# Scores of an eight-level scan: 64x64 column tiles in two bursts per head, six homes for mixed operands, a compact score tile

## The reference

```python
def step(state, inp):
    qb, kb, fb, vb = inp
    b = jnp.cumsum(fb, axis=2)
    b_last = b[:, :, -1:, :]
    inter = jnp.einsum('nhtk,nhkv->nhtv', qb * jnp.exp(b), state)
    diff = b[:, :, :, None, :] - b[:, :, None, :, :]
    decay = jnp.exp(jnp.where(incl, diff, -jnp.inf))
    scores = jnp.einsum('nhtk,nhsk,nhtsk->nhts', qb, kb, decay)
    intra = jnp.einsum('nhts,nhsv->nhtv', scores, vb)
    new_state = (jnp.exp(b_last[:, :, 0, :, None]) * state
                 + jnp.einsum('nhsk,nhsv->nhkv', kb * jnp.exp(b_last - b), vb))
    return new_state, inter + intra
...
o2 = hgrn2_chunk_scan(jnp.concatenate([qh, rev(qh)], axis=0),
                      jnp.concatenate([k_f, rev(k_b)], axis=0),
                      jnp.concatenate([logf_f, rev(logf_b)], axis=0),
                      jnp.concatenate([vh, rev(vh)], axis=0))
o = o2[:B] + rev(o2[B:])
```

## Time and profile before

| | |
|---|---|
| median of 3 runs | 1886.5 us (1885.9 to 1886.76) |
| the profiled execution's time | 1885.56 us |
| its span | 1883.7 us |
| TensorE products busy | 1853.5 us, 98% of the span |
| TensorE weight loads | 1602.5 us, 85% |
| VectorE | 1401.9 us, 74% |
| ScalarE | 1042.4 us, 55% |
| GpSimdE | 331.4 us, 18% |
| chain that ended last | PE 83%, DVE 13%, ACT 2%, issue 2% |
| L2036 (level steps) in that chain | 2% |

### The profile page before, as it was taken

The page is one execution under the profiler, slowest core; times in us unless marked ns, Lnnn a source line. Parts: engine busy times, 40 slices in busy tenths (PEclk is TensorE's granted clock), DMA queues, the critical chain, the costliest instruction groups (busy, mean ns, idle before and its releaser), DMA issues.

```text
span 1883.7 us, 32317 instructions
## 1 busy us (share of the span) xinstructions
PE 1853.5 (98%) x11238; PEld 1602.5 (85%) x11238; DVE 1401.9 (74%) x2658; ACT 1042.4 (55%) x1817; POOL 331.4 (18%) x145
## 2 busy tenths in 40 slices
PE   9999999999999999999999999999999999999998
PEld 7877887788888889999999998888888888888887
DVE  7785566667655568898997678977999976666666
ACT  6666455656644466667555555565665543333333
POOL 0000000000000000000000168886777400000000
PEclk9999999999999999999999999999999999999999
DMA  6624655443455544443445445554444455555554
GB/s 217 224 78 148 216 174 178 145 146 124 146 189 189 187 147 157 147 135 124 136 145 175 155 143 181 186 189 152 162 157 161 155 187 192 196 191 191 196 193 156
DMA packets 86157, 314.11 MB, mean 167 GB/s; under 512 B 9568, under 2 KB 9696, under 8 KB 85856
## 3 DMA queue, kind: packets, MB, share of 16 engines
q1 hardware_dynamic: 86048, 312.65, 49.2%
HBM read 311.56 MB, written 1.05 MB: 166 GB/s over the span
## 4 chain that ended last, share of the span: by engine, by line
PE 83%; DVE 13%; ACT 2%; issue 2%; DMA 0%; SPq 0%; DVEq 0%; ACTq 0%
PE ps L424 24%; PE ps L409 14%; PE ps L2735 11%; PE ps L290 6%; PE ps L1967 6%; PE ps L2739 6%; PE ps L2537 3%; DVE wsplit L273 3%; PE ps L819 2%; PE ps L2036 2%; PE ps L2923 1%; DVE sq L2979 1%; PE ps L440 1%; ACT wsplit L267 1%; DVE work L2300 1%
## 5 line engine op out<-in xcount | busy, mean ns | idle before, releaser
L267 ACT ACTIVATE wsplit<-ring 128x1024 fp32r<-128x1024 f32 x572 | 603.8, 1059 | 450.5 <-PE ps L424 265.4
L273 DVE TENSOR_TENSOR wsplit<-ring,wsplit 128x1024 fp32r<-128x1024 f32 x440 | 541.5, 1235 | 304.8 <-ACT wsplit L267 303.8
L424 PE MATMUL ps<-wsplit,gsplit 128*128 128x512 f32 x1992 | 456.5, 390 | 0.0
L424 PEld LDWEIGHTS ps<-wsplit,gsplit 128*128 128x128 f32 x1992 | 373.2, 188 | 81.3 <-issue 4.0
L273 POOL TENSOR_TENSOR wsplit<-ring,wsplit 128x1024 fp32r<-128x1024 f32 x132 | 317.2, 2404 | 664.5 <-ACT wsplit L267 664.2
L2735 PE MATMUL ps<-hsplit,wsplit 128*128 128x512 f32 x1024 | 368.6, 403 | 0.0
L409 PE MATMUL ps<-wsplit,hsplit 128*128 128x512 f32 x1248 | 298.1, 394 | 4.5 <-DVE wsplit L273 3.4
L2739 PE MATMUL ps<-hsplit,wsplit 128*128 128x256 f32 x1024 | 286.4, 280 | 0.0
L409 PEld LDWEIGHTS ps<-wsplit,hsplit 128*128 128x128 f32 x1248 | 231.6, 188 | 55.5 <-DVE wsplit L273 7.3
L290 PE MATMUL ps<-hsplit,wsplit 128*128 128x256 f32 x1956 | 253.6, 287 | 2.6 <-DVE hsplit L340 1.5
L290 PEld LDWEIGHTS ps<-hsplit,wsplit 128*128 128x128 f32 x1956 | 239.8, 191 | 10.4 <-issue 4.5
(11 more groups left out here) (346 smaller groups left out, 1900.3 us busy)
## 6 DMA issues: line engine op xcount, KB each, us to landing
ring<-in_weights SPq DMA_DIRECT2D x572, 512.0 KB, 3.3
work<-in_weights SPq DMA_DIRECT2D x8, 512.0 KB, 5.8
...
```

Source lines behind the costliest of these rows:

```text
L267: act.activation(wsplit[:, n % RING, 0, :], slab(s), ACT.Copy).then_inc(S("split", "lead"), 1)
L273: eng.tensor_tensor(wsplit[:, n % RING, 1, :], slab(s), wsplit[:, n % RING, 0, :], ALU.subtract).then_inc(S("split", RESTS[stream][0]), 1)
L424: mm = pe.matmul(YR[:, tt, half * 512:(half + 1) * 512], gsplit[:, slot, b, tt * P:(tt + 1) * P], wsplit[:, n, a, half * 512:(half + 1) * ...
```

## The change

- The eight steps within the quadrants' halves (diagonal, levels 0 to 5, and level 6, which pairs the halves) are products of 64 keys and 64 queries: four for a step, two for each half of PSUM's partitions, into 128 columns. Steps 0 to 3 lie in bank 3, steps 4 to 7 in bank 5. TensorE does them in two bursts of 16 products, before slot 3 and before slot 6. The step across stays as it was, now before slot 7, into bank 3.
- Mixed operands have six homes instead of two, the four old half-homes as four whole ones and two more in `yb`.
- VectorE collects steps 0 to 6 in a 128x(2x64) tile `near`, the first with a copy, the others under 64-wide masks: two after growth 4, one after growth 5, one after growth 6, and three at the head's end, where the last keep was.
- ScalarE copies `near` into `sT` (two instructions, one for each half of the partitions), then step 7 directly out of PSUM (two more), then the step across.

```diff
@@ -181,7 +181,9 @@
     tab = carve(N_TABLE - N_EYES)
     sm = carve(N_SMALL)
     hT = carve(KC, T)
-    level_masks = carve(LEVELS, P, dt=I32)
+    level_masks = carve(LEVELS - 1, HD, dt=I32)
+    near = carve(2, HD)
+    pos[0] += LEVELS * P - LEVELS * HD - HD
     filt_sum = carve(2, D)
     filt_dif = carve(2, D)
     sub = carve(16, P)
@@ -1933,9 +1935,26 @@
     qa, kb = qakb[:, 0, :, :], qakb[:, 1, :, :]
     totals = [forget.rearrange("p a t -> p (a t)")] + [carve(3 * (T >> l)) for l in range(1, LEVELS)]
     sT = carve(TT, T)
-    mixed = merged[:, 0:4, :].rearrange("p (b x) t -> p b x t", b=2)
+    mixed = [merged[:, 2 * b:2 * b + 2, :] for b in range(4)] + [yb[:, 4 + 2 * b:6 + 2 * b, :] for b in range(2)]
     hv = yb[:, 0:4, :].rearrange("p (t a) n -> p t (a n)", t=TT)
-    diag = strided(sT, 0, [[T + P, 2], [1, P]])
+
+    def half(h2):
+        return slice(HD * h2, HD * h2 + HD)
+
+    def quadrants(keys, queries):
+
+        return strided(sT, HD * queries, [[T + P, 2], [1, HD]], HD * keys, HD)
+
+    across_bank = ps[:, 3, 0:T]
+
+    def level_tiles(k):
+        return ps[:, 3 + 2 * (k // 4), k % 4 * P:(k % 4 + 1) * P].rearrange("p (a c) -> p a c", a=2)
+
+    def mix_home(h, l):
+        return mixed[(h * (LEVELS + 1) + l) % len(mixed)]
+
+    def level_steps(h, k):
+        return h * (LEVELS + 2) + k + 1
     hy = carve(3, T + 2)
     u = carve(T)
     assert pos[0] <= NKEYS * T
@@ -2020,24 +2039,41 @@
     def hyena_input(k):
         return ps[:, (0, 0, 1, 7)[k], (k % 2) * T:(k % 2 + 1) * T]
 
-    def hgrn_head_tensor(pe, st, h):
-        steps = h * (LEVELS + 2)
-        for k in range(LEVELS + 2):
-            dst = ps[:, 3 + 2 * (k % 2), 0:T].rearrange("p (a c) -> p a c", a=2)
+    def near_levels_tensor(pe, st, h, k0):
+
+        for k in range(k0, k0 + 4):
             if k == 0:
                 pe.wait_ge(S(st, "prep"), h + 1)
-            else:
-                pe.wait_ge(S(st, "mixed"), h * (LEVELS + 1) + k)
-            if k >= 2:
-                pe.wait_ge(S(st, "kept"), h * (LEVELS + 1) + (k - 1))
-            q_, k_ = (qh, ksum) if k == 0 else (mixed[:, (k - 1) % 2, 0, :], mixed[:, (k - 1) % 2, 1, :])
+                pe.wait_ge(S(st, "mixed"), h * (LEVELS + 1) + 3)
+            if k == 4:
+                pe.wait_ge(S(st, "mixed"), h * (LEVELS + 1) + LEVELS)
+            q_, k_ = (qh, ksum) if k == 0 else (mix_home(h, k - 1)[:, 0, :], mix_home(h, k - 1)[:, 1, :])
             for a in range(2):
-                b = 1 - a if k > LEVELS else a
-                mm = pe.matmul(dst[:, a, :], k_[:, a * P:(a + 1) * P], q_[:, b * P:(b + 1) * P], start=True, stop=True)
+                for h2 in range(2):
+                    keys, queries = a * P + HD * h2, a * P + HD * (1 - h2 if k == LEVELS else h2)
+                    mm = pe.matmul(level_tiles(k)[half(h2), a, :], k_[:, keys:keys + HD], q_[:, queries:queries + HD],
+                                   start=True, stop=True)
             mm.then_inc(S(st, "level"), 1)
+
+    def across_level_tensor(pe, st, h):
+        pe.wait_ge(S(st, "mixed"), (h + 1) * (LEVELS + 1))
+        pe.wait_ge(S(st, "kept"), h * LEVELS + 4)
+        q_, k_ = mix_home(h, LEVELS)[:, 0, :], mix_home(h, LEVELS)[:, 1, :]
+        for a in range(2):
+            mm = pe.matmul(across_bank[:, a * P:(a + 1) * P], k_[:, a * P:(a + 1) * P], q_[:, (1 - a) * P:(2 - a) * P],
+                           start=True, stop=True)
+        mm.then_inc(S(st, "level"), 1)
+
+    def hgrn_head_tensor(pe, st, h):
+        for k in range(LEVELS + 2):
+            if k == 3:
+                near_levels_tensor(pe, st, h, 0)
+            if k == 6:
+                near_levels_tensor(pe, st, h, 4)
+            if k == 7:
+                across_level_tensor(pe, st, h)
             hgrn_slot(pe, st, h, k)
         pe.wait_ge(S(st, "scores"), h + 1)
-        pe.wait_ge(S(st, "kept"), (h + 1) * (LEVELS + 1))
         pe.wait_ge(S(st, "v_sb"), h // 4 + 1)
         if h:
             pe.wait_ge(S(st, "o_sb"), h)
@@ -2072,10 +2108,11 @@
             act.wait_ge(S(st, "prep"), h + 1)
         else:
             act.wait_ge(S(st, "grown"), h * LEVELS + l)
-        if h or l > 1:
-            act.wait_ge(S(st, "level"), h * (LEVELS + 2) + (l if l > 1 else l - 1))
+        before = h * (LEVELS + 1) + l - len(mixed)
+        if before >= 0:
+            act.wait_ge(S(st, "level"), level_steps(before // (LEVELS + 1), before % (LEVELS + 1) + 1))
         for x_ in range(2):
-            ins = act.activation(strided(mixed, (l % 2 * 2 + x_) * T, [[2 * size, n], [size, 2], [1, size]]),
+            ins = act.activation(strided(mix_home(h, l), x_ * T, [[2 * size, n], [size, 2], [1, size]]),
                                  strided(qakb, x_ * 2 * T, [[2 * size, n], [T + size, 2], [1, size]]), ACT.Copy)
         ins.then_inc(S(st, "mixed"), 1)
 
@@ -2139,8 +2176,14 @@
                 hyena_stage_scalar(act, "hyena", 0, 0)
         if last:
             hyena_stage_scalar(act, "hyena", 0, 1)
+        act.wait_ge(S(st, "kept"), (h + 1) * LEVELS)
+        for h2 in range(2):
+            act.activation(quadrants(h2, h2), near[half(h2), :, :], ACT.Copy)
+        act.wait_ge(S(st, "level"), (h + 1) * (LEVELS + 2) - 1)
+        for h2 in range(2):
+            act.activation(quadrants(h2, 1 - h2), level_tiles(LEVELS)[half(h2), :, :], ACT.Copy)
         act.wait_ge(S(st, "level"), (h + 1) * (LEVELS + 2))
-        act.activation(strided(sT, P, [[1, T]]), ps[:, 3, 0:T], ACT.Copy).then_inc(S(st, "scores"), 1)
+        act.activation(strided(sT, P, [[1, T]]), across_bank, ACT.Copy).then_inc(S(st, "scores"), 1)
         leads_beside(act, st, h, LEVELS)
         leads_beside(act, st, h, LEVELS + 1)
         if not last:
@@ -2198,14 +2241,12 @@
 
     def keep_vector(v, st, h, k):
 
-        v.wait_ge(S(st, "level"), h * (LEVELS + 2) + k + 1)
-        if k > LEVELS - 2:
-            v.wait_ge(S(st, "kept"), h * (LEVELS + 1) + k)
-        src = ps[:, 3 + 2 * (k % 2), 0:T].rearrange("p (a c) -> p a c", a=2)
-        if k == 0:
-            ins = v.tensor_tensor(diag, src, eye.unsqueeze(1).to_broadcast([P, 2, P]), ALU.mult)
+        v.wait_ge(S(st, "level"), level_steps(h, 3 if k < 4 else LEVELS))
+        if k:
+            v.wait_ge(S(st, "kept"), h * LEVELS + k)
+            ins = v.copy_predicated(near, level_masks[:, k - 1, :].unsqueeze(1).to_broadcast([P, 2, HD]), level_tiles(k))
         else:
-            ins = v.copy_predicated(diag, level_masks[:, k - 1, :].unsqueeze(1).to_broadcast([P, 2, P]), src)
+            ins = v.tensor_copy(near, level_tiles(k))
         ins.then_inc(S(st, "kept"), 1)
 
     def hgrn_head_vector(v, own, st, h):
@@ -2221,7 +2262,8 @@
             if l < LEVELS - 1:
                 own(v.tensor_tensor(strided(totals[l + 1], 0, [[n, 3], [1, n]]), strided(t_, 0, [[nt, 3], [2, n]]),
                                     strided(t_, 1, [[nt, 3], [2, n]]), ALU.mult))
-            keep_vector(v, st, h, l)
+            for k in {4: (0, 1), 5: (2,), 6: (3,)}.get(l, ()):
+                keep_vector(v, st, h, k)
             if l:
                 rests_beside(v, st, h, l - 1)
             if l == 1:
@@ -2233,7 +2275,8 @@
         else:
             hyena_gates_vector(v, own, "hyena", 0)
         rests_beside(v, st, h, LEVELS - 1)
-        keep_vector(v, st, h, LEVELS)
+        for k in range(4, LEVELS):
+            keep_vector(v, st, h, k)
         if last:
             hyena_u_vector(v, own, "hyena", 0)
         rests_beside(v, st, h, LEVELS)
@@ -3322,8 +3365,8 @@
     out = np.zeros((P, N_TABLE), np.float32)
     for k, (a, n) in TABLE.items():
         out[:, a:a + n] = t[k]
-    s, c = np.meshgrid(pp, pp, indexing="ij")
-    m = [((s >> (l + 1)) == (c >> (l + 1))) & ((s >> l) != (c >> l)) for l in range(LEVELS)]
+    s, c = np.meshgrid(pp % HD, np.arange(HD), indexing="ij")
+    m = [((s >> (l + 1)) == (c >> (l + 1))) & ((s >> l) != (c >> l)) for l in range(LEVELS - 1)]
     return out, np.stack(m, 1).astype(np.int32)
```

## The result

The kernel with the change takes 1900.27 us (median of 4 runs, 1899.34 to 1901.21), the kernel before, run beside it, 1886.2 us. The ratio is 1.0073 (95% interval 1.0061 to 1.0085): slower, by some 14 us. The prediction said slower, with 1892.9 us and a range up to 1898.5; the sign held, the size did not (+14.1 where +6.4 stood), and the time lies above the range.

The account below looks back on a forecast made before the run. T bounds the kernel before; after the change a V, A, V circle does. Heads 0 to 3 +0.2, heads 4 to 6 +5.1, last head +1.1 give +6.4 us: 1892.9 us, range 1887.0 to 1898.5.

Parts of the forecast that it names:

- The circle: At a head's end, V's keeps, A's copies, score copy, lead, V's rest: five-slab heads 21.2 us for 19.50; chance 0.56.
- T's side of the sum: Eight level steps a head (3.7 us) become two bursts (2.5 us); T saves 1.1 to 1.2 us a head.
- T stays the bound: In the heads, the V and A circle stays under T's time: 8.8 us gained, 1877.7 us; chance 0.10.
- the circle closes cheaper: With V's keeps and A's copies at lower bounds, a head is 0.5 to 0.7 us shorter: 1888 to 1889; chance 0.12.
- the two halves do not overlap: T's 64-column records run one by one: a burst takes 2.16 us, total 1895 to 1897 us; chance 0.04.
- the price of A's copies: At a head's end, A's four new 64-partition copies take 4 x 0.19 us, then the score copy 0.29.
- heads 4 to 6: The five-slab heads each get 1.70 us longer, 3 x 1.70 = 5.1 us.
- The six-slab heads: Heads 1 to 3 take 21.75 us against 21.95, head 0 uses up that gain; heads 0 to 3 together +0.2 us.
- The last head: In the four-slab head T itself is last, behind level 6's mix: +1.1 us, bounds 0 and 1.5.
- The third rival: T's waits before the second burst in heads 4 to 7 drop the clock: +3.5 us, 1896.4 us; chance 0.18.
- The upper end of the range: Keeps as slow as now and A's copies at 0.39 us add 0.8 or more a head, to 1898.5 us.
- What would show it: Trace signs in the heads: waits of T, V and A, head lengths, bursts of 1.0 to 1.2 us, clock under 1.00.

Follow-up runs that it names:

- run 1: The changed kernel with A's lead issued before the wait for the seventh keep instead of behind the score copy: 1892.36 us, ratio 1.0029 to the kernel before.
- run 6: The changed kernel with V's three last keeps between the next head's gates and its preparation, except in the last head: 1890.8 us, ratio 1.0023.
- run 8: The changed kernel with V's three last keeps before the next head's preparation and T's bursts a slot later (before slots 4 and 7): 1888.01 us, ratio 1.0007.
- run 4: The changed kernel with A's four copies ordered by half (near 0, step 0, near 1, step 1): 1897.74 us, ratio 1.0069.
- run 5: The changed kernel without A's two copies of step 7's scores and the wait ahead of them, so no replacement for the change: 1895.54 us, ratio 1.0049.
- run 10: Changed kernel with lead first, keeps early, bursts late; last head alone: second burst before slot 8, across step after slab products, keeps before hyena gates: 1884.41 us.
- run 2: The changed kernel with eight extra float32 products on T ahead of each second burst: 1899.25 us, ratio 1.0075.
- run 7: The changed kernel with V's three last keeps before the next preparation, plus eight float32 filler products on T before each second burst: 1895.91 us, ratio 1.0048.
- run 9: The changed kernel with lead before the seventh keep's wait, V's last keeps before the next preparation, and T's bursts a slot later: 1885.62 us, ratio 0.9998.

## Why the prediction was right in sign and wrong in size

**The circle was right.** The walk from V's keeps over A's copies, score copy and lead to V's rest is the path that the trace shows, and runs 1, 6 and 8 shorten the heads by opening it. T's side of the sum held too: two bursts at 1.29 us for eight steps at 0.45 save 1.0 to 1.1 us a head, the halves do overlap (32 records in 1.01 us), and none of it is seen, as said. The rivals "T stays the bound", "the circle closes cheaper" and "the two halves do not overlap" fall.

**The step that failed is the price of A's copies** ("pitch 0.19 as L2143's next starts 0.1 before its end"). It carried an overlap that was read behind the old score copy over to four new copies of half the partitions. Of the walked 21.20 and the measured 22.07 us of a five-slab head:

| part of the circle | walked | measured in head 6 | more |
|---|---|---|---|
| first growth to the first of the three last keeps | 16.88 | 17.08 | 0.20 |
| three keeps, until A starts | 1.05 | 1.14 | 0.09 |
| four copies, until the score copy starts | 0.76 | 1.21 | 0.45 |
| score copy, until the lead starts | 0.29 | 0.40 | 0.11 |
| lead, until V's rest starts | 1.09 | 1.10 | 0.01 |
| rest, until the next growth | 1.13 | 1.14 | 0.01 |

0.56 of the 0.87 us are A's five copies: the four new ones lie 0.30 apart and not 0.19, and the lead 0.40 behind the score copy and not 0.29. By the pattern of run 4 that is five instructions held back by about 0.1 each. Run 5 shows that the measured pitch is what counts (0.56 to 0.58 for two of them, in six of seven heads). Over heads 4 to 6 the forecast had 5.1 us and it is 7.75 (66.55 for 58.80); the copies are 1.7 of the 2.65 missed. The 0.2 us ahead of the keeps and the 0.1 in them are measured and not explained.

**The six-slab heads** are the larger miss: +0.2 was forecast for heads 0 to 3 and it is +3.2 (89.74 for 86.55). The same circle is in them (at the end of head 2 V's rest waits 2.74 us for A's lead, and the five copies take 1.61 us, where 1.05 was walked): heads 1 to 3 came at 22.45, 0.7 above the walked 21.75, and head 0 at +1.7 where the forecast let it use up the 0.6 us gained by the three others. The term near zero was the difference of two near-equal lengths, and it carried the error of the copies four times over: 2.2 of the 3.0 us missed there.

**The last head** was forecast at +1.1 and came at +1.5 (18.2 for 16.6). The forecast let T itself be last. T's own part came as walked, 5.57 us from the burst's first load to the end of the slab loads (894.54 to 900.11) where 5.65 stood. But then T waits 0.55 us for A's score copy (L2081 above), and A had waited 1.18 for the seventh keep. Run 10 gives 1.5 us back by moving T's work into its waits and V's three keeps ahead, in a kernel with other heads before it; the two were not tried apart.

**The clock.** The third rival said that it falls and adds 3.5 us. It did fall, in heads 5 and 6, and run 2 shows that there it added nothing, as the circle over the lead was longer than T at half clock. Once that circle is opened by the early keeps (run 6), the fall holds heads 5 and 6 at 22.0: run 7 removes it, and 1.4 us a head with it. A circle that no row of the change shows as the bound stood right below the one that it does. In the last head the change shows no fall; runs 1, 5, 8 and 9, where a stretch at half clock lies in it, have that head at 18.9 to 20.4 us, but no run separates the clock from their other edits there.

Together: heads 0 to 6 came 10.9 us longer (5.3 forecast), the last 1.5 (1.1 forecast), 12.5 for 6.4. The copies are 3.9 (seven times 0.56) of the 5.6 us missed in heads 0 to 6. The other 1.6 us of the medians' 14.1 were not traced to a cause. The upper end of the range, 1898.5, is the forecast and 0.8 us in each of seven heads, from the four copies at 0.39. That alone just covers the miss in these heads. It left nothing for keeps as slow as before, though the sentence names them, nor for the score copy, the last head and what lies outside the heads, and the time came 1.8 us above it.

**What would show it**, point by point: T's wait before the second burst is 2.45 us in head 6 (2 to 3 said); V's rest waits 2.7 (about 2 said); A waits 4.4 for the seventh keep (3 or more said); five-slab heads 22.1 (21.2 said), six-slab 22.45 (21.5 to 21.8 said); a burst from first load to next slab product 1.08 (1.0 to 1.2 said); and the clock did fall, the sign of the third rival.
